# Index-query splits ahead of the angles, chunks multiplied hi parts first, and a small softmax moved to a later stage

## What is computed

```python
def dsa_mixer(x, cos, sin, w_in, w_o):
    proj = x @ w_in                                   # 1024 x 2120
    q, k, v, iq, ik, iw = jnp.split(proj, A_SPLITS, axis=-1)
    q, k, iq, ik = (partial_rotary(t, cos, sin) for t in (q, k, iq, ik))
    s = jnp.einsum('bqhd,bsd->bqhs', iq_b, ik) * IDX_DIM ** -0.5
    score = jnp.einsum('bqh,bqhs->bqs', iw_b, jax.nn.relu(s))
    _, sel = lax.top_k(score, 64)                     # then attention over the chosen keys
...
lb_soft = jax.nn.softmax(hgrn_lb_logits, axis=0)      # 2 x 1024, used only by the last mixer
lower_bounds = jnp.cumsum(lb_soft, axis=0) - lb_soft[0:1]
```

## Time and profile before

| | us |
|---|---|
| median of three runs | 1254.51 |
| lowest and highest | 1254.41, 1255.26 |
| the profiled execution's own time | 1254.74 |
| its span in the trace | 1253.0 |
| PE busy | 1234.9 |
| DVE busy | 855.4 |
| ACT busy | 593.2 |
| POOL busy | 93.1 |

### The profile page before, as it was taken

How to read it: one execution, slowest core, us unless ns; L and a number is a source line. 1 busy time by engine, 2 the same in 40 slices (tenths; PEclk the granted TensorE clock), 3 DMA queues, 4 the chain that set the end, 5 groups by cost and what they waited for, 6 DMA issues and landing times.

```text
span 1253.0 us, 19256 instructions
## 1 busy us (share of the span) xinstructions
PE 1234.9 (99%) x8277; PEld 1065.4 (85%) x8277; DVE 855.4 (68%) x919; ACT 593.2 (47%) x725; POOL 93.1 (7%) x226
## 2 busy tenths in 40 slices
PE   8989999999999999999999999999999999999998
PEld 7878888888888888888988888888998888888887
DVE  6787766666666676666786666667577667666675
ACT  5674443444743543443664443345562445434434
POOL 4351000001000200000201000001000100000000
PEclk9999999999999999999999999999999999999999
DMA  8423665555643765554624665555554346655642
GB/s 278 149 88 128 210 201 178 192 200 147 211 136 119 250 193 180 198 198 135 231 76 171 199 201 179 191 201 201 185 172 160 111 144 234 201 180 190 201 142 94
DMA packets 131268, 221.06 MB, mean 176 GB/s; under 512 B 6984, under 2 KB 99424, under 8 KB 131184
## 3 DMA queue, kind: packets, MB, share of 16 engines
q1 hardware_dynamic: 128160, 209.83, 50.4%
q0 software_dynamic: 3024, 10.01, 2.7%
HBM read 218.77 MB, written 1.05 MB: 175 GB/s over the span
## 4 chain that ended last, share of the span: by engine, by line
PE 83%; DVE 7%; ACT 4%; DMA 2%; issue 2%; POOL 1%; SPq 0%; ACTq 0%; POOLq 0%; DVEq 0%
PE ps L607 18%; PE ps L757 18%; PE ps L759 9%; PE ps L584 9%; PE ps L585 9%; PE ps L586 9%; PE ps L718 4%; DVE wlo L1781 3%; ACT whi L1322 2%; PE ps L771 2%; ACT rot L1347 1%; DMA raw<-in_mlp_w_up 1%; DMA raw<-in_ffn_w_in 1%; PE ps L928 1%; DVE buf L1860 1%
## 5 line engine op out<-in xcount | busy, mean ns | idle before, releaser
L1781 DVE TENSOR_TENSOR wlo<-raw,whi 128x2048 fp32r<-128x2048 f32 (+3 forms) x203 | 452.1, 2241 | 174.6 <-ACT whi L1322 173.5
L1322 ACT ACTIVATE whi<-raw 128x2048 fp32r<-128x2048 f32 (+3 forms) x203 | 376.9, 1869 | 67.6 <-DMA raw<-in_hgrn_w_in 19.6
L757 PE MATMUL ps<-xhl,whi 128*128 128x512 f32 x1088 | 271.4, 391 | 0.0
L757 PEld LDWEIGHTS ps<-xhl,whi 128*128 128x128 f32 x1088 | 198.3, 188 | 37.3
L607 PE MATMUL ps<-whi,xhl 128*128 128x512 f32 (+1 forms) x864 | 212.8, 379 | 3.7 <-DVE wlo L1781 1.8
L607 PEld LDWEIGHTS ps<-whi,xhl 128*128 128x128 f32 x864 | 152.0, 188 | 34.6 <-DVE wlo L1781 2.6
L584 PE MATMUL ps<-whi,hh 128*128 128x512 f32 x432 | 169.0, 391 | 0.0
L585 PE MATMUL ps<-whi,hl 128*128 128x512 f32 x432 | 168.6, 390 | 0.0
L586 PE MATMUL ps<-wlo,hh 128*128 128x512 f32 x432 | 168.1, 389 | 0.0
L759 PEld LDWEIGHTS ps<-xhl,wlo 128*128 128x128 f32 x1088 | 148.4, 190 | 10.6
L759 PE MATMUL ps<-xhl,wlo 128*128 128x256 f32 x1088 | 151.7, 282 | 0.0
(11 more groups left out here) (331 smaller groups left out, 1303.9 us busy)
## 6 DMA issues: line engine op xcount, KB each, us to landing
raw<-in_ffn_w_in SPq DMA_DIRECT2D x44, 1024.0 KB, 5.1
raw<-in_mlp_w_up SPq DMA_DIRECT2D x32, 1024.0 KB, 5.4
raw<-in_mlp_w_down SPq DMA_DIRECT2D x32, 1024.0 KB, 4.9
raw<-in_ffn_w_down SPq DMA_DIRECT2D x22, 1024.0 KB, 4.8
raw<-in_hgrn_w_in SPq DMA_DIRECT2D x16, 1024.0 KB, 5.3
raw<-in_b_w_in SPq DMA_DIRECT2D x12, 1024.0 KB, 5.2
raw<-in_ple_w_gate SPq DMA_DIRECT2D x8, 1024.0 KB, 6.0
raw<-in_a_w_in SPq DMA_DIRECT2D x6, 1024.0 KB, 5.2
```

The costliest lines, as they stand in the source:

```text
L757: mm(bank(b + f), w[0][:, kk, P * f : P * f + P], xhl[:, kk, :, :].rearrange("p a n -> p (a n)"), start=(kk == 0), stop=False)
L1322: a.activation(whi[:, slot, 0:w], raw[:, slot, 0:w], ACT.Copy).then_inc(s["hi_done"], 1)
L1781: v.tensor_tensor(wlo[:, slot, 0:w], raw[:, slot, 0:w], whi[:, slot, 0:w].bitcast(F32), ALU.subtract).then_inc(s["lo_done"], 1)
```

## The change

Three things are done.

1. PE works through chunks 0 to 3 by a new function, `index_queries`. It multiplies the products that need only `whi` first (x_hi x w_hi and x_lo x w_hi), after a wait for `hi_done`, and then x_hi x w_lo after `lo_done`. The first tile's products of chunk 0 stand ahead of the transposes of the second tile of x; `keep_fed` there has 6 transposes in place of 16. The transpose of the row vectors (`vrow`) goes from after chunk 1 to after chunk 3.
2. ACT and DVE issue the splits of chunks 1 to 3 (ACT: 1 to 4) ahead of the angles and sines.
3. The softmax of the lower bounds is worked out in the GLA stage: three DVE operations before `gate_logs`, ACT's exponential after `gate_exps`, seven DVE operations after `ahead(first["gla_r"])`.

```diff
@@ PE
+            def index_queries(q, tiles, parts):
+                n = first["dsa_iq"] + q
+                w = weights(n, 2, 512)
+                for part, w_part in parts:
+                    if w_part:
+                        take(n)
+                    else:
+                        pe.wait_ge(s["hi_done"], n + 1)
+                    for tt in tiles:
+                        for kk in range(2):
+                            if kk == 0 and q % 2 == 0 and not w_part:
+                                pe.wait_ge(s["turn_lo" if part else "turn_hi"], 2 * tt + q // 2 + 1)
+                            last = mm(bank(2 + tt), (xh, xl)[part][:, 2 * q + kk, P * tt : P * tt + P], w[w_part][:, kk, :],
+                                      start=(q == 0 and (part, w_part) == (0, 0) and kk == 0), stop=(q == 3 and w_part == 1 and kk == 1))
+                return last
             keep_fed(12)
             turn_tile(T_X0, x, 0)
-            keep_fed(16)
+            keep_fed(6)
+            index_queries(0, [0], [HI, LOW_X])
             turn_tile(T_X0, x, 1)
-            take(first["dsa_iq"])
...
+            index_queries(0, [0], [LOW_W])
+            index_queries(0, [1], [HI, LOW_X, LOW_W]).then_inc(s["w_done"], 1)
             for q in range(1, 4):
-                by_rows(first["dsa_iq"] + q, 2, 512, 2 * q, KD, [(tt, slice(0, 512), bank(2 + tt)) for tt in range(TT)])
...
+                index_queries(q, range(TT), [HI, LOW_X, LOW_W]).then_inc(s["w_done"], 1)
+            pe.wait_ge(s["vrow_landed"], 64)
+            nc.tensor.transpose(ps[:, 6, 0:V_ROWS], vrow[:, :], ident[0:V_ROWS, 0:V_ROWS]).then_inc(s["vrow_turned"], 1)
@@ ACT
-            until(first["dsa_iq"] + 1)
+            until(first["dsa_small"])
             for w, (sn, cs) in enumerate(((sinA, cosA), (sinM, cosM))):
                 act.wait_ge(s["angle_done"], w + 1)
                 a.activation(sn[:, :, :], cs[:, :, :], ACT.Sin)
                 a.activation(cs[:, :, :], cs[:, :, :], ACT.Sin, scale=0.5).then_inc(s["sines_done"], 1)
-                until(first["dsa_iq"] + 3)
...
-            act.wait_ge(s["lb_diff"], 1)
-            a.activation(lbv[:, 1:3, :], lbv[:, 1:3, :], ACT.Exp).then_inc(s["lb_exp"], 1)
@@ ACT, GLA stage
             a.activation(expo[0][:, 0:1008], expo[0][:, 0:1008], ACT.Exp, scale=1.0 / 16.0).then_inc(s["gate_exps"], 1)
+            act.wait_ge(s["lb_diff"], 1)
+            a.activation(lbv[:, 1:3, :], lbv[:, 1:3, :], ACT.Exp).then_inc(s["lb_exp"], 1)
@@ DVE
-            until(first["dsa_iq"] + 1)
+            until(first["dsa_iq"] + 3)
...
                 v.tensor_scalar(cs[:, :, :], cs[:, :, :], PI_MAX, -PI_MAX, ALU.min, ALU.max).then_inc(s["angle_done"], 1)
-                until(first["dsa_iq"] + 2 + w)
-            until(first["dsa_iq"] + 3)
+                until(first["dsa_small"])
...
             until(first["dsa_q"])
-            dve.wait_ge(s["vcol_done"], 1)
...
-            step(v.tensor_scalar(one, e1, -1.0, 1.0, ALU.mult, ALU.add))
             until(first["dsa_q"] + 1)
@@ DVE, GLA stage: three operations ahead of gate_logs, seven after ahead(gla_r)
             ahead(first["gla_low"])
+            dve.wait_ge(s["vcol_done"], 1)
...
+            v.tensor_tensor(e1, l1, mx, ALU.subtract).then_inc(s["lb_diff"], 1)
             dve.wait_ge(s["tail_done"], 1)
...
             ahead(first["gla_r"])
+            dve.wait_ge(s["lb_exp"], 1)
+            step(v.tensor_tensor(sm, e0, e1, ALU.add))
...
             decay_end(T_GLA, [0], 256, 64, first["gla_r"], first["gla_o"])
```

More of the change, by code:

```diff
@@ L967, in keep_fed @@
                     nc.tensor.transpose(ps[:, 1, P * (q % 4) : P * (q % 4) + P], ident[:, :], ident[:, :])
+            def index_queries(q, tiles, parts):
[13 more added lines that the diff above has]
+                return last
+            HI, LOW_X, LOW_W = (0, 0), (1, 0), (0, 1)
             keep_fed(12)
             turn_tile(T_X0, x, 0)
-            keep_fed(16)
+            keep_fed(6)
+            index_queries(0, [0], [HI, LOW_X])
             turn_tile(T_X0, x, 1)
-            take(first["dsa_iq"])
-            for tt in range(TT):
-                pe.wait_ge(s["turn_lo"], 2 * tt + 2)
-                last = rows(first["dsa_iq"], 2, 512, 0, KD, [(tt, slice(0, 512), bank(2 + tt))])
-            last.then_inc(s["w_done"], 1)
+            index_queries(0, [0], [LOW_W])
+            index_queries(0, [1], [HI, LOW_X, LOW_W]).then_inc(s["w_done"], 1)
             for q in range(1, 4):
-                by_rows(first["dsa_iq"] + q, 2, 512, 2 * q, KD, [(tt, slice(0, 512), bank(2 + tt)) for tt in range(TT)])
-                if q == 1:
-                    pe.wait_ge(s["vrow_landed"], 64)
-                    nc.tensor.transpose(ps[:, 6, 0:V_ROWS], vrow[:, :], ident[0:V_ROWS, 0:V_ROWS]).then_inc(s["vrow_turned"], 1)
+                index_queries(q, range(TT), [HI, LOW_X, LOW_W]).then_inc(s["w_done"], 1)
+            pe.wait_ge(s["vrow_landed"], 64)
+            nc.tensor.transpose(ps[:, 6, 0:V_ROWS], vrow[:, :], ident[0:V_ROWS, 0:V_ROWS]).then_inc(s["vrow_turned"], 1)
             n = first["dsa_small"]
@@ L2159, in _ @@
             ahead(first["gla_low"])
+            dve.wait_ge(s["vcol_done"], 1)
+            l0, l1 = vcol[:, V_LB : V_LB + 8], vcol[:, V_LB + 8 : V_LB + 16]
+            mx, e0, e1, sm, one = (lbv[:, i, :] for i in range(5))
+            step(v.tensor_tensor(mx, l0, l1, ALU.max))
+            v.tensor_tensor(e0, l0, mx, ALU.subtract)
+            v.tensor_tensor(e1, l1, mx, ALU.subtract).then_inc(s["lb_diff"], 1)
             dve.wait_ge(s["tail_done"], 1)
@@ L2180, in _ @@
             ahead(first["gla_r"])
+            dve.wait_ge(s["lb_exp"], 1)
+            step(v.tensor_tensor(sm, e0, e1, ALU.add))
+            step(v.reciprocal(sm, sm))
+            v.tensor_tensor(e0, e0, sm, ALU.mult)
+            step(v.tensor_tensor(e1, e1, sm, ALU.mult))
+            step(v.tensor_tensor(e1, e0, e1, ALU.add))
+            step(v.tensor_tensor(e1, e1, e0, ALU.subtract))
+            step(v.tensor_scalar(one, e1, -1.0, 1.0, ALU.mult, ALU.add))
             decay_end(T_GLA, [0], 256, 64, first["gla_r"], first["gla_o"])
```

12 lines of the change are left out of this document (removed).

## The result

| | before | changed |
|---|---|---|
| median of the runs compared, us | 1254.47 (21 runs) | 1257.09 (21 runs) |
| lowest and highest, us | 1253.56, 1255.72 | 1254.78, 1258.48 |
| the profiled execution's own time, us | 1254.74 | 1254.78 |
| its span, us | 1253.0 | 1253.1 |

What follows compares the result with a forecast made beforehand. PE, busy nearly throughout at full clock, was taken as the bound. From 1254.74 us, 1.67 gained at chunk 5 and 2.82 lost to POOL's stall gave 1255.89, or 1255.7 for the median; range 1252.8 to 1256.8.

Steps and rivals of the forecast that it cites:

- Chunks 0 to 3 in hi-first order; PE at chunk 5: First-stage chunk loop: PE begins chunk 5 at 24.6 us after waiting about 1 us for DVE, 1.7 us earlier.
- POOL's collision takes it back: Before the index transposes: POOL, excluded by DVE's lo splits, signals index_rotated at 38.85; PE starts there 1.15 us later than before.
- POOL keeps up: Rival at the index transposes: POOL finishes in time, PE goes on at 36.0, 1252.8 us; chance 0.20 with half-way cases.
- The clock falls in the new gap: Rival: PE's 2.8 us stand before the index transposes lowers the clock, costing 2.2 us, 1257.9 in all; chance 0.06.
- `keep_fed`, the table load, the softmax in both places: First stage and GLA stage: fewer `keep_fed` transposes, the later exponential table load and the moved softmax each cost 0.

Runs made afterwards that it cites:

- the last base recording: Changed kernel with DVE's wait for index_rotated ahead of its later lo splits and two wide products filling PE's attention gap: 1252.69 us, ratio 0.9984.
- the moved wait: Changed kernel with DVE's wait for index_rotated put ahead of the lo splits of chunks 8 to 10, so POOL finishes first: 1252.88 us, ratio 0.9988.
- the two later sets: The changed kernel, unchanged, run again twice, on two chips: 1256.0 us (ratio 1.0011) and 1256.08 us (ratio 1.001).
- PE's order alone: Kernel before with only PE's part of the change (`index_queries`, six `keep_fed`, later `vrow`): 1255.41 us, ratio 1.0012.
- the fastest kernel: Changed kernel with earlier index_rotated wait, filled attention gap, and table M's angles, sines and cosines moved behind chunk 6's splits: 1251.38 us, ratio 0.9974.

## Why the prediction was wrong, point by point

- *Chunks 0 to 3 in hi-first order; PE at chunk 5.* Right. The chunk loop ended where forecast (chunk 1 at 12.04, chunk 4's product from 20.47), and DVE's lo split 5 held PE. The recording has 23.93 in place of 24.6 and a wait of 0.41 in place of 1 us, because chunk 3 landed early; the last base recording, with a later landing, has 24.57 and 1.07. What I took for a constant was one landing, 10.2 us in one recording.
- *POOL's collision takes it back.* Right in mechanism, and shown by the moved wait. The transposes came at 37.81, not 38.85, in the first recording, and at 38.30, 38.37, 38.90 in those of the same programs or nearly so. Over all runs the size holds: at clock 1.0 the changed kernel has a median of 1255.3 (7 runs of the two later sets), before 1253.94 (55 runs), so the stall's net price is 1.4 us, for 1.15 forecast. That it comes so near is in part luck. With ACT's start on chunk 3 at the forecast's 13.54, line 478 would end at 38.4 by the 24.9 us above, so POOL's working was 0.4 us too long; and the recording of before that I measured from was one of the later ones (transposes at 37.69; 37.08, 37.11 and 37.71 in three recordings of the kernel before with one small edit each). The reason was incomplete: the prediction says that lo split 6 follows at once because its hi part is ready, and behind it I thought of the new order on DVE and ACT, as the expectation for PE's order alone says, while PE's order alone does it.
- *POOL keeps up.* Did not happen by itself; with POOL let through first it gave 1252.9, for the rival's 1252.8.
- *The clock falls in the new gap, chance 0.06.* This is the step that failed: the sum puts the clock at nothing, and the runs have it at 2.0 us of the median. I weighed it by one row, a wait of 1.10 us that was passed at full clock, and took silence of the forty digits for a full clock in all executions. It falls there in four of seven recordings. In the runs of the result 7 of 21 have the clock of one fall (0.998) and 8 that of two (0.997), one in each gap. The price of 2.2 us was near: it is 1.7. With it the median works out, since the run at the median is one of those at 0.998: 1253.94 + 1.4 + 1.7 = 1257.0, for 1257.09. Behind which gap the fall lies in such a run is not known, as it has no trace. In the two later sets of runs, where fewer had a low clock, the kernel had 1256.0 and 1256.08, inside the range; so whether the range holds hangs on how often the clock falls in a set of runs, and nothing here says what decides that. By the Trainium skill (TensorE: Matmul & The Clock Gate, Part 1) an idle array gets half the clock and a busy one the full clock again; the rows agree, 0.50 behind the gap and 1.00 after it.
- *`keep_fed`, the table load, the softmax in both places.* Cost nothing, as forecast; the runs of the softmax alone (ratio 0.9999) and of 14 transposes (1256.15 us, beside 1256.0 with six) bear it out.
- *The same 1.7 us per fall in the attention* was in the profile before as a wait of PE that I did not look at, since it is the same in both kernels. It spreads both kernels' times and hid behind the median.

## What to carry to other kernels

Before moving an engine earlier, list what it releases: here PE's progress brought DVE's two-input operations onto POOL's work, and 0.8 us of POOL's became 5.1. Where the slack of a helper engine is a matter of a single operation's start, order it by a wait instead of hoping for it. And price an idle gap of PE of about 2 us at more than its length: look at the granted clock in fine stretches just behind it, and at the mean clock of every run, since a single recording may be one that escaped.

## What was unexpected of the hardware

- Behind a gap of 2.2 us, and of 1.88 us in the attention, the clock was halved, and it stayed half for 3.41 us while PE was busy; behind the same gap other executions kept the full clock.
- The landing of the same transfer, chunk 3, lets ACT start between 12.75 and 13.91 in the recordings of kernels with the change, with nothing changed ahead of it in the programs of SP and ACT.
- A float32 product of 128 x 512 took 0.89 us (4.45 us for five), 3.6 times a product of 128 x 512 in the reduced format (1.98 us for eight, 0.25 each).
- With 38 PE instructions more at 36 us PE stood still for 1.53 us in front of 968.04; whether and how the one brings the other was not settled.
- Two of nine runs of the fastest kernel have a mean clock of 0.999 and are the fastest of all (1250.95 and 1250.63), so that reading alone is no proof of a fall. The clock is also half at the end of the span, for 0.64 us in that kernel's recording; 1.25 us of it would be enough for 0.999, which no recording shows.
